# Tile stride and weight-buffer offset in an fp32r transformer kernel: 1024 bytes for 1088, and 64 bytes of pad

## The reference, cut to what matters

```python
zl = hl @ w_in[l] + b_in[l]                       # 256 tokens
zkv = hc @ w_in[l, :, K_OFF:G_OFF] + ...          # 256 context tokens, keys and values only
xl = xl + mod_l[2][:, None, :] * mixer_output(zl, y_na_l, *branch_params)
xl = xl + mod_l[5][:, None, :] * sq_relu_ffn(hl2, w_ff1[l], b_ff1[l], w_ff2[l], b_ff2[l])
```

## The kernel before, in words

| stage | activations | columns | units x matmuls |
|---|---|---|---|
| modulation of the first four vectors | vectors | 512 | no units |
| keys and values | `AH`/`AL` and `CH`/`CL` in turn | 256 | 32 x 48 |
| queries, gated unit, convolution input | `AH`/`AL` | 256 | 80 x 24 |
| gates | `AH`/`AL` | 256 | 96 x 24 |
| branch outputs, between the gates | `BH`/`BL` | 256 | 48 x 24 |
| `w_o` | `YH`/`YL` | 256 | 32 x 24 |
| first feed-forward matrix | `AH`/`AL` | 258 | 128 x 24 |
| second feed-forward matrix | `YH`/`YL` | 256 | 128 x 24 |
| attention input | `AH`/`AL` | 272 | 128 x 24 |
| attention output | `YH`/`YL` | 272 | 32 x 24 |
| pooling input, first half | `AH`/`AL` | 272 | 32 x 24 |
| pooling input, second half | `AH`/`AL` from token 16 on | 256 | 32 x 24 |
| pooling groups (L894, L895, L898) | `YH`/`YL` | 256 | 8 x 24 |
| pooling output | `AH`/`AL` | 256 | 32 x 24 |

## Time and profile before

### The profile page before, as it was taken

How to read it: one execution, slowest core, us unless ns; L and a number is a source line. 1 busy time by engine, 2 the same in 40 slices (tenths; PEclk the granted TensorE clock), 3 DMA queues, 4 the chain that set the end, 5 groups by cost and what they waited for, 6 DMA issues and landing times.

```text
span 2867.4 us, 51278 instructions
## 1 busy us (share of the span) xinstructions
PE 2733.7 (95%) x21330; PEld 2574.7 (90%) x21330; DVE 1915.3 (67%) x2964; ACT 1224.9 (43%) x1801; POOL 219.4 (8%) x212
## 2 busy tenths in 40 slices
PE   5889999899999899999999999999999998979996
PEld 1279977699999899999999999999999997979996
DVE  6655567789999777875554555677656665477564
ACT  2122244444434544544443444564444444444452
POOL 4000011200003200100000000021000000220011
PEclk8999999999999999999999999999999999989998
DMA  7766643264877687775555555554444443535553
GB/s 259 267 211 219 210 145 115 84 221 155 268 238 256 199 278 254 262 230 194 188 186 183 183 185 185 183 192 155 155 133 159 148 156 108 188 110 177 185 190 103
DMA packets 163991, 539.01 MB, mean 188 GB/s; under 512 B 31024, under 2 KB 35120, under 8 KB 163632
## 3 DMA queue, kind: packets, MB, share of 16 engines
q1 hardware_dynamic: 163760, 535.73, 56.7%
HBM read 533.57 MB, written 2.10 MB: 187 GB/s over the span
## 4 chain that ended last, share of the span: by engine, by line
PE 84%; DVE 10%; issue 2%; DMA 1%; ACT 1%; SPq 1%; POOL 0%; POOLq 0%; ACTq 0%; DVEq 0%
PE ps L472 26%; PE ps L477 25%; PE ps L474 25%; DVE lo L1529 3%; PE ps L573 2%; PE ps L626 1%; PE ps L645 1%; DMA raw<-in_w_mod 1%; DVE macc L1646 1%; DVE CV L1789 1%; PE ps L634 1%; DVE row L2075 1%; DVE macc L1517 0%; DVE macc L1520 0%; PE ps L800 0%
## 5 line engine op out<-in xcount | busy, mean ns | idle before, releaser
L472 PE MATMUL ps<-AH,hi 128*128 128x256 f32 (+2 forms) x4480 | 1289.0, 288 | 13.5 <-DVE AL L2151 13.5
L477 PE MATMUL ps<-AH,lo 128*128 128x256 f32 (+2 forms) x4480 | 1277.6, 285 | 19.6 <-DVE lo L1529 19.6
L474 PE MATMUL ps<-AL,hi 128*128 128x256 f32 (+2 forms) x4480 | 1274.1, 284 | 0.0
L923 ACT ACTIVATE hi<-raw 128x1024 fp32r<-128x1024 f32 x808 | 850.5, 1057 | 935.0 <-PE ps L477 498.4
L1529 DVE TENSOR_TENSOR lo<-raw,hi 128x1024 fp32r<-128x1024 f32 x808 | 977.9, 1224 | 191.5 <-ACT hi L923 190.3
L472 PEld LDWEIGHTS ps<-AH,hi 128*128 128x128 f32 x4480 | 850.6, 190 | 45.3 <-issue 34.5
L477 PEld LDWEIGHTS ps<-AH,lo 128*128 128x128 f32 x4480 | 851.3, 190 | 23.0 <-DVE lo L1529 22.8
L474 PEld LDWEIGHTS ps<-AL,hi 128*128 128x128 f32 x4480 | 850.2, 190 | 0.8
L472 PE MATMUL ps<-YH,hi 128*128 128x256 f32 (+1 forms) x1536 | 434.0, 283 | 6.5 <-DVE YL L2086 6.5
L477 PE MATMUL ps<-YH,lo 128*128 128x256 f32 (+1 forms) x1536 | 435.1, 283 | 0.0
L474 PE MATMUL ps<-YL,hi 128*128 128x256 f32 (+1 forms) x1536 | 435.1, 283 | 0.0
(11 more groups left out here) (245 smaller groups left out, 2606.6 us busy)
## 6 DMA issues: line engine op xcount, KB each, us to landing
raw<-in_w_ff SPq DMA_DIRECT2D x256, 512.0 KB, 4.2
raw<-in_w_in SPq DMA_DIRECT2D x208, 512.0 KB, 4.4
raw<-in_w_mod SPq DMA_DIRECT2D x192, 512.0 KB, 4.6
raw<-in_w_ain SPq DMA_DIRECT2D x128, 512.0 KB, 3.5
raw<-in_w_pin SPq DMA_DIRECT2D x64, 512.0 KB, 3.5
raw<-in_w_o SPq DMA_DIRECT2D x32, 512.0 KB, 4.6
raw<-in_w_aout SPq DMA_DIRECT2D x32, 512.0 KB, 3.5
raw<-in_w_pout SPq DMA_DIRECT2D x32, 512.0 KB, 3.5
```

The costliest lines, as they stand in the source:

```text
L472: e.matmul(b.ap[:, o], hi[:, k, :], xh, start=start and k + i == 0, stop=False, skip_group_check=many)
L474: e.matmul(b.ap[:, o], hi[:, k, :], xl, start=False, stop=False, skip_group_check=many)
L477: mm = e.matmul(b.ap[:, o], los[j % NSPLIT][:, k, :], xh, start=False, stop=stop and k == KU - 1, skip_group_check=many)
L923: e.activation(his[u % NSPLIT][:, :, :], raws[i % NRAW][:, :].rearrange("p (k m) -> p k m", k=KU), ACT.Copy).then_inc(s_hi, 1)
```

## The change

Nothing is added to or taken from the work: the same instructions in the same order with the same waits. Two things about addresses change.

- A view `dense` packs the first 16 x 256 elements of `AH`, `AL`, `YH` and `YL` with 256 elements from one `k` to the next in place of 272. All writers and readers of the stages with exactly 256 tokens use it (keys and values, queries to gates, `w_o`, second feed-forward matrix, pooling groups, pooling output). The stages with 258 and 272 columns, and the second half of the pooling input, keep the step of 1088 bytes.
- A tile `pad` of 64 bytes stands between `AL` and `raw0`. So `raw`, `hi`, `lo` and everything declared from the left behind them, `BH` and `BL` too, begin 64 bytes later; `AH`, `AL`, `CH`, `CL`, `YH`, `YL` stay.

```diff
         AH, AL = sb("AH", [128, 16, L], F32R), sb("AL", [128, 16, L], F32R)
+
+        sb("pad", [128, 16])
         raws = [sb(f"raw{i}", [128, KU * 128]) for i in range(NRAW)]
...
+        def dense(t):
+            return t[:, :, :].rearrange("p k t -> p (k t)")[:, 0:16 * T].rearrange("p (k t) -> p k t", t=T)
+
+        A1H, A1L, Y1H, Y1L = (dense(t) for t in (AH, AL, YH, YL))
...
-            lat = lambda k: [(AH[:, k, 0:T], AL[:, k, 0:T], slice(0, T))]
-            both = lambda k: [(AH[:, k, 0:T], AL[:, k, 0:T], slice(0, T)), (CH[:, k, :], CL[:, k, :], slice(T, 2 * T))]
+            lat = lambda k: [(A1H[:, k, :], A1L[:, k, :], slice(0, T))]
+            both = lambda k: [(A1H[:, k, :], A1L[:, k, :], slice(0, T)), (CH[:, k, :], CL[:, k, :], slice(T, 2 * T))]
...
-            mixed = lambda k: [(YH[:, k, 0:T], YL[:, k, 0:T], slice(0, T))]
+            mixed = lambda k: [(Y1H[:, k, :], Y1L[:, k, :], slice(0, T))]
...
-                e.activation(YH[:, m, 0:T], x[:, 0:T], ACT.Copy).then_inc(s_fh, 1)
+                e.activation(Y1H[:, m, :], x[:, 0:T], ACT.Copy).then_inc(s_fh, 1)
...
-                e.tensor_tensor(YL[:, m, 0:T], x[:, 0:T], YH[:, m, 0:T].bitcast(F32), ALU.subtract).then_inc(s_fl, 1)
+                e.tensor_tensor(Y1L[:, m, :], x[:, 0:T], Y1H[:, m, :].bitcast(F32), ALU.subtract).then_inc(s_fl, 1)
```

More of the change, by code:

```diff
@@ L893, in _ @@
                                 e.wait_ge(s_al, 48 + kt + 1)
-                            e.matmul(b.ap[:, 0:T], hi[:, 4 * mi + k, :], YH[:, kt, 0:T], start=(k == 0), stop=False)
-                            e.matmul(b.ap[:, 0:T], hi[:, 4 * mi + k, :], YL[:, kt, 0:T], start=False, stop=False)
+                            e.matmul(b.ap[:, 0:T], hi[:, 4 * mi + k, :], Y1H[:, kt, :], start=(k == 0), stop=False)
+                            e.matmul(b.ap[:, 0:T], hi[:, 4 * mi + k, :], Y1L[:, kt, :], start=False, stop=False)
                             if mi == k == 0:
                                 e.wait_ge(s_lo, j + 1)
-                            mm = e.matmul(b.ap[:, 0:T], lo[:, 4 * mi + k, :], YH[:, kt, 0:T], start=False, stop=(k == 3))
+                            mm = e.matmul(b.ap[:, 0:T], lo[:, 4 * mi + k, :], Y1H[:, kt, :], start=False, stop=(k == 3))
                         mm.then_inc(s_unit if mi else s_grp, 1)
@@ L995, in modulate @@
                     for k in range(4 * g, 4 * g + 4):
-                        for hi in (AH, CH):
+                        for hi in (A1H, CH):
                             e.wait_ge(s_mx, n + 1)
@@ L1204, in mixed_out @@
                     e.wait_ge(s_bl, 24)
-                e.activation(YH[:, m, 0:T], tmp[m % 3][:, 0:T], ACT.Copy, scale=0.5).then_inc(s_yh, 1)
+                e.activation(Y1H[:, m, :], tmp[m % 3][:, 0:T], ACT.Copy, scale=0.5).then_inc(s_yh, 1)
                 yield
@@ L1451, in pool_out @@
                     e.wait_ge(s_unit, used["w_aout", 15, 0])
-                e.activation(YH[:, m, 0:T], tmp[2 + m % 2][:, NM:L], ACT.Copy).then_inc(s_ph, 1)
+                e.activation(Y1H[:, m, :], tmp[2 + m % 2][:, NM:L], ACT.Copy).then_inc(s_ph, 1)
                 yield
@@ L1459, in grp_out @@
                     e.wait_ge(s_unit, used["w_pin", 31, 0])
-                e.activation(AH[:, m, 0:T], tmp[(4 + m) % 7][:, 0:T], ACT.Copy).then_inc(s_gh, 1)
+                e.activation(A1H[:, m, :], tmp[(4 + m) % 7][:, 0:T], ACT.Copy).then_inc(s_gh, 1)
                 yield
@@ L1616, in modulate @@
                         yield
-                        for v, (hi, lo) in enumerate(((AH, AL), (CH, CL))):
+                        for v, (hi, lo) in enumerate(((A1H, A1L), (CH, CL))):
                             e.wait_ge(s_hx, n + v + 1)
@@ L1866, in branch_out @@
                 e.wait_ge(s_yh, m + 1)
-                e.scalar_tensor_tensor(out=YL[:, m, 0:T], in0=x[:, 0:T], scalar=0.5, in1=YH[:, m, 0:T].bitcast(F32),
+                e.scalar_tensor_tensor(out=Y1L[:, m, :], in0=x[:, 0:T], scalar=0.5, in1=Y1H[:, m, :].bitcast(F32),
                                        op0=ALU.mult, op1=ALU.subtract).then_inc(s_yl, 1)
@@ L2196, in pool_out @@
                 e.wait_ge(s_ph, m + 1)
-                e.tensor_tensor(YL[:, m, 0:T], x[:, NM:L], YH[:, m, 0:T].bitcast(F32), ALU.subtract).then_inc(s_al, 1)
+                e.tensor_tensor(Y1L[:, m, :], x[:, NM:L], Y1H[:, m, :].bitcast(F32), ALU.subtract).then_inc(s_al, 1)
             def grp_out(m):
@@ L2213, in grp_out @@
                 e.wait_ge(s_gh, m + 1)
-                e.tensor_tensor(AL[:, m, 0:T], x[:, 0:T], AH[:, m, 0:T].bitcast(F32), ALU.subtract).then_inc(s_al, 1)
+                e.tensor_tensor(A1L[:, m, :], x[:, 0:T], A1H[:, m, :].bitcast(F32), ALU.subtract).then_inc(s_al, 1)
             units(1, 5)
```

## The result

The changed kernel takes 2849.56 us (median of 4 runs, 2847.83 to 2853.54), beside 2871.88 us for the kernel before in the same comparison; the ratio is 0.9922 with a 95% interval of 0.9905 to 0.9939. That is 22.3 us faster. The forecast was 2822.7 us, 49 us faster, and the range ended at 2849.0. So the sign was right, and the size was not.

The account below looks back on a forecast made before the run. TensorE's matmul-to-matmul step was taken as the bound. Stage gains 8.6 + 8.6 + 7.8 + 3.8 + 15.4 + 1.0 + 3.8 = 49.0 us took the median from 2871.7 to 2822.7 us, range 2806 to 2849.

Parts of the forecast that it names:

- TensorE's step: Whole kernel: time from one matmul's start to the next, with TensorE busy 95% of the span, sets the end.
- the remainder of the difference: 256-column matmuls: activation address minus weight-slice address, by 256, sets the pace; frozen at 192 it gives 113.3 ns, not 118.3.
- the bound of 1 ns: 258- and 272-column stages and second half of pooling input: no change, at most 1 ns a matmul, 8 us either way.
- slow entry: BH units in the gates: 48 entries lose their two 120 ns steps, worth 0.6 us, of which 0.4 is kept.
- a rule of the Trainium skill: TensorE's independent read ports would make operand places irrelevant: no effect, 2871.7 us, as in the no-effect rival, chance 0.11.
- the 4.8 us of the forecast: Pooling groups gain 1.0 us and pooling output 3.8 us from faster 256-column steps.
- The term that failed: 256-column streams using the dense view: step falls from about 118.3 to 113.3 ns, some 5.0 ns a matmul.
- The deductions: Gain lowered from 54.3 to 49.0 us, mainly 4.1 us for VectorE between 690 and 1000 us, also a GpSimd chain.
- B: Rival: absolute place or the slice's 512 bytes also counts, so about half the streams gain; 2847 us, chance 0.12.
- C: Rival: freezing pins all 256-column matmuls to a bad place at 120 ns; 18 us slower, 2890 us, chance 0.06.
- The range: Whole kernel: 2806 to 2849 us, including the half-gain rival; about 2 in 10 left outside.
- The keys and values before: Keys and values: 1536 matmuls go from 118.9 to 113.3 ns, gaining 8.6 us.

Follow-up runs that it names:

- run with a start at 192 bytes: Changed kernel without the pad, dense view beginning 192 bytes into its tensor (AH, AL, YH, YL at remainder 192; CH, CL at 0): 2859.33 us, ratio 0.9947.
- run with the ending at 64: Changed kernel, last first-feed-forward unit before each second-feed-forward block in k order 3, 4, 5, 6, 7, 0, 1, 2: 2836.36 us, ratio 0.9869.
- second profile: The changed kernel run and profiled once more, nothing altered: 2850.17 us, ratio 0.9923.
- four endings: Changed kernel (walking stream before the second feed-forward matrix ends at remainder 128), and reordered k ending at 192, 64, 0: 2849.56, 2850.18, 2836.36, 2849.43 us.
- runs with added breaks: Changed kernel with short matmuls or transpositions before or inside second-feed-forward blocks, once also elsewhere: 2850.71, 2844.05, 2849.65, 2852.86 us.

## Why the prediction was wrong

**What held.** TensorE's step was the bound, no wait took the place of the gain, and the remainder of the difference decides, not the absolute place (the run with a start at 192 bytes, the one other place tried). The 258- and 272-column stages stayed within 0.4 ns of their steps, so the bound of 1 ns was wide enough. `BH` lost its slow entry: behind a gate at the fast pace its first steps are 113 and 114 ns. The prediction weighed a rule of the Trainium skill (page "SBUF — State Buffer", section "Who interferes with whom": TensorE never waits on anyone, and its two read ports are independent) and what would follow from it, that where the operands lie would not matter. That consequence is contradicted by 120.0, 118.7 and 113.3 ns for one shape at three remainders. The groups and the pooling output gained the 4.8 us of the forecast to within 0.1.

**The term that failed** is the step after the change: "The bounds of that step ... I take 113.3, the only level row with this shape and this remainder." It was not the only level row. `BH` in the kernel before has slow units too: six of its 48. Those at 959 and 992 us came behind a late `lo`, the one at 950 us where the granted clock came back from 0.5 to 1.00, and those at 866, 929 and 1055 us behind a few short matmuls of another kind. Timeline of PE before, 15 matmuls:

```profile
960.01 0.28 PE L472 MATMUL ps<-BH,hi 128*128 128x256 f32 x1
...
961.78 0.28 PE L472 MATMUL ps<-BH,hi 128*128 128x256 f32 x1
```

1.77 / 15 = 118.0 ns, at remainder 192, beside the 113.3 of rows 3. I had read one unit of `BH` and taken it for all 48. With two paces the term would have been 0.5 or 5.0 ns, and the stages had to be priced by how they are entered. The cost by stage is in the table above: 13.8 us for the second feed-forward matrix, 1.8 for `w_o`, and 11.9 up to the gates' end. There `BH` itself got worse: it had been fast in 42 of 48 units, entered from a walking stream each time, and was slow in 19 of 48 after, since it now takes over whatever pace the gates have. The run with the ending at 64 shows the term as it was forecast where the way in is good: the second feed-forward matrix then takes 113.3 ns and 15.2 us less than before.

**The deductions** (5.3 us, most of it for VectorE in the gates) are not shown to be right or wrong. The mean step in the gates fell from 118.1 to 115.0 ns, some three fifths of what was assumed, and between 690 and 1000 us the waits on `lo` were 9.8 us before and 10.6 after. Up to the gates' end the faster steps alone were worth 16.9 us and the stretch gained 13.1; the rest went into waits, short breaks and more time at the granted clock of 0.5 (33 us there beside 25 before). In the second profile it was 15.7 and 14.7.

**The rivals.** B (part of it, 2847 us) came nearest in time, by luck, since it gave another reason: neither the absolute place nor the 512 bytes of a slice. C, a frozen place that is bad, is real at remainder 0: without the pad the kernel is at 2888 us, close to the 2890 that C named. It did not occur at 192.

**The range** was drawn from a step that was either 113.3 or not. It ended at 2849.0, half a microsecond short, because case B stood in it with nothing around it. The keys and values before were also read a little low: 118.9 ns in one stretch of 36 matmuls, 119.2 over the stage.

## What to carry to other kernels

Where matmuls and weight loads run back to back, compare the steps of equal shapes over all their occurrences, not over one unit; if a shape runs at two paces without a wait, look at the remainder of moving operand minus weights. A remainder with a fast pace may have a slow one too, and then the way into the stage (the last few matmuls before it) is part of the tuning: here the order of eight `k` was worth 13.8 us, while padding without the dense view gave some 3 us, and the dense view without the pad cost 14. Count on a gain of that kind only where a profile shows the fast pace in that very stage and the stage is entered from a walking stream without waits.

## What the runs showed of the hardware that I had not expected

- One shape (128x128 weights, 256 columns, float32) has the mean steps 120.0 ns at remainder 0, 118.7 at 128, 118.3 at 224, from 117.3 to 120.0 at 160, and two level ones, 113.3 and 117.8, at 192 and at 64, all at a granted clock of 1.00.
- The two paces hold over whole blocks of 32 units (768 matmuls) and are thrown over by as little as eight one-column matmuls: 11 of 12 turns did so in the first profile, and in 80 turns of eight profiles the fast pace was lost each time, and the slow one left whenever the pause was 930 to 934 ns and not when it was 928.
- From a stream of walking remainders without waits the outcome is repeatable (with four endings, four blocks each, all blocks of a kernel alike, and the changed kernel the same in two profiles). Why an ending at 64 leads to the fast pace and the other three to the slow one stays open: no run shows what inside TensorE or the memory carries the state.
- Executions of one kernel can differ in their paces: the two profiles of the changed kernel differ in the gates. That the scatter of its times (2847.8 to 2853.5 us for four runs) comes from there is not shown; the kernel before scatters as much (2869.4 to 2879.6 us for 19 runs beside the runs with added breaks).
